# Two transformer blocks on one core: 258 columns, earlier splits, sums by fours and reordered steps

## Chip, core and metric

One core of one Trainium2 chip runs the kernel in a single launch. The metric is the device time of that launch in microseconds (us); lower is better. Three runs of the kernel before gave 1582.75, 1585.87 and 1586.20 us, so their median is 1585.87 us.

## What is computed

A sequence of 16 meta tokens and 256 input tokens of 1024 features passes through a first block of two layers. Then the 256 tokens pass through a second block of two more. All numbers are fp32. Cut to the shapes that matter:

```python
hs = concat([meta_tokens, x])                      # 272 tokens, first_block
for i in range(2):
    mix = gated_deltanet(...) if i == 0 else mlstm(...)
    hs = hs + rms_norm(mix, norm_w[i, 1])
    u = causal_depthwise_conv(rms_norm(hs, norm_w[i, 2]) @ w_up[i], conv_w[i]) + conv_b[i]   # 3 taps
    f = (silu(u[..., :2816]) * u[..., 2816:]) @ w_down[i]
    hs = hs + rms_norm(f, norm_w[i, 3])
x = hs[:, 16:]                                     # the meta tokens are dropped here
for layer in range(2):                             # second_block
    y = short_conv_mixer | swa_sink_attention  if layer == 0  else  gla_mixer | mla_mixer
    x = layer_norm(ALPHA * x + y @ w_out)
    x = layer_norm(ALPHA * x + (silu(x @ w_gate) * (x @ w_up)) @ w_down)
```

Nothing after the second layer's mixer mixes tokens except the convolution of three taps. For its 256 tokens the last projections of that layer need at most two tokens ahead of them.

## The kernel before

Activations lie with features on the partitions and tokens in the columns: 272 columns in the first block (`T1`), 256 in the second (`T2`), or 258 (`TB`) where two columns more carry a bias. All weights come as one stream of 412 blocks of 128 x 1024 fp32, loaded through SyncE's queue into a ring of four slots (`raw`). For each block ScalarE makes a rounded high part (`split_hi`, L375, `whi`) and VectorE the rest (`split_lo`, L380, `wlo`). TensorE then forms each fp32 product from three fp32r matmuls (`three`, L399 to L401): high by high, high by low, low by high. A block is 24 matmuls.

There are sixteen phases: an input projection (kind "tiles", one block gives one PSUM bank of 128 output features) and an output projection (kind "wide", each block adds to all eight banks) for each mixer and each feed-forward part. In order they are gdn_in, gdn_out, up0, down0, ml_in, ml_out, up1, down1, ev_in, ev_out, up2, down2, od_in, od_out, up3, down3. The names stand in the table `PHASES`.

The order on each engine is written out by hand, and semaphores join the engines. What the change touches:

- **The wave.** After a norm, `pe_tiles` starts the first three tiles of the next input projection while VectorE and ScalarE still produce its eight input chunks (`next_dve`, `next_act`, or `ln_dve`, `ln_act` in the second block). In the wave TensorE also sums squares over features with fp32 matmuls against ones (`sums_pe`, L565). VectorE first adds the squares in pairs (`pair_sum`, L621), so there are four such matmuls. `act_scale` (L505, L507) makes the scale from their sum.
- **The fourth and fifth tile.** The fourth tile's block is split inside the wave (`fourth`). The fifth's is split in `ffn_act`/`ffn_dve`, `ml_gates_act`/`ml_gates_dve` or `od_tile_act`/`od_tile_dve`, that is four tiles ahead (`TAIL = 4`).
- **The feed-forward pairs.** `ffn_act` and `ffn_dve` treat tiles two by two: scale, convolution taps (L690, L698) or bias, SiLU, product. GpSimd forms the gated product and its two parts (`ffn_pool`).
- **The mixers of the second block.** `even_pe`/`even_act`/`even_dve` lay tiles 6 to 17 of ev_in between the steps of the windowed attention. `odd_pe`/`odd_act`/`odd_dve`/`odd_pool` do so for od_in, the gated linear attention (gla) and the latent attention (mla).
- **The output rows.** `pe_wide` goes block by block. Each block passes all eight banks in order, and in the first block each bank is waited for (`bank_ready`), since the mixer's last steps still read some.

Of the kernel before, what the change touches and what calls it, by code (L numbers as in the profile page):

```python
# [42 lines left out]
OD_TILES = tuple(range(12, 17)) + (4, 5, 6, 7, 2, 3, 0, 1, 8, 9, 10, 11)  # L43
# [241 lines left out]
def build(nc, stream, params, consts, mla, hs_in, out, table):  # L285
# [98 lines left out]

    def split_all(engine, split, phase, lo=0, count=None):
# [17 lines left out]
    def pe_tiles(pe, phase, g0, name, count=None, meanwhile=lambda k: None):  # L403

        b0, n = FIRST_BLOCK[phase], count or COUNT[phase]
        T = width(phase)
        mm = nc.tensor.matmul

        for k in range(KC + 1):
            if k < KC:  # L410
                w = slice(k * P, (k + 1) * P)
                pe.wait_ge(*S("norm", "act").at(f"{name}_hi{k}"))
                for j in range(AHEAD):
                    o, s = rhs_out(g0 + j, phase), (b0 + j) % SLOTS
                    if k == 0:
                        pe.wait_ge(block_split, b0 + j + 1)
                        pe.wait_ge(bank_free, g0 + j + 1)
                    mm(o, whi[:, s, w], xs[:, k, 0:T], start=(k == 0), stop=False)  # L418
                    mm(o, wlo[:, s, w], xs[:, k, 0:T], start=False, stop=False)  # L419
            if k:  # L420
# [3 lines left out]
                for j in range(AHEAD):  # L424
                    last = mm(rhs_out(g0 + j, phase), whi[:, (b0 + j) % SLOTS, w], xs[:, KC + k - 1, 0:T], start=False, stop=(k == KC))  # L425
# [3 lines left out]
        def tile(j, i=0):  # L429
# [3 lines left out]
            for k in range(KC):  # L433
                last = three(rhs_out(g, phase), (b0 + j) % SLOTS, k, xs[:, k, 0:T], xs[:, KC + k, 0:T], k == 0, k == KC - 1)
# [27 lines left out]

    def pe_wide(pe, phase, g0, ready, bank_ready=lambda pe, b: None):

        b0, n = FIRST_BLOCK[phase], COUNT[phase]
        T = T1 if b0 < FIRST_BLOCK["ev_in"] else T2
        half = {"ml_out": range(ML_HALF, ML_HALF + 16), "od_out": OD_HALF}.get(phase, range(48))
        def rows(k, i=None):
# [4 lines left out]
            for m in range(8):  # L473
# [3 lines left out]
                last = three(rhs_out(g0 + m, phase), (b0 + k) % SLOTS, m, hf[:, half[at] if i is None else at, 0:T], hf[:, half[lo] if i is None else lo, 0:T], k == 0, k == n - 1)  # L477
                if i is None and k == n - 1 and m < 7:
                    last.then_inc(*S("wide", "pe").mark(f"{phase}_m{m}"))
            last.then_inc(block_used, 1)  # L480
# [8 lines left out]
        else:  # L489
            for k in range(n):  # L490
# [61 lines left out]
    def keep_clock(pe, g, n, lo=0):  # L552

        pe.wait_ge(bank_free, g + 1)
        for _ in range(n):
            nc.tensor.matmul(bank[g % 8][:, 0:T2], hf[:, lo, 0:P], hf[:, lo + 1, 0:T2], start=True, stop=True)

    def sums_pe(pe, name, src, g, parts, T):

        for m, first, last_one in parts:  # L560
# [4 lines left out]
            last = nc.tensor.matmul(bank[g % 8][:, 0:T], ones, ap, start=first, stop=last_one)  # L565
# [3 lines left out]
    def post_src(name):  # L569
        def src(m):  # L570
            return ("dve", f"{name}_sum{FIRST_SUM - 1}", sq[:, 0, :]) if m == 0 else ("act", f"{name}_{m}", sq[:, m, :])
        return src

    def post_pe(pe, name, g):
        sums_pe(pe, name, post_src(name), g, ((3, True, False), (4, False, False), (0, False, False), (5, False, False),
                                              (6, False, False), (7, False, True)), T1)
        keep_clock(pe, g + 1, 16, ML_HALF if name == "post2" else 0)

    def post_act(act, name, g, phase):
        for m in range(KC):  # L580
            wide_done(act, phase, m)
            nc.scalar.activation(sq[:, m, :], bank[(g - 8 + m) % 8][:, 0:T1], ACT.Square).then_inc(*S("norm", "act").mark(f"{name}_{m}"))  # L582
        split_hi(act, used_after(phase) + AHEAD - 1)
        act.wait_ge(*S("norm", "pe").at(name))
        nc.scalar.activation(rs[:, 1, :], bank[g % 8][:, 0:T1], ACT.Ln, bias=eps_1, scale=1.0 / D).then_inc(*S("norm", "act").mark(f"{name}_ln"))
        act.wait_ge(*S("norm", "act").at(f"{name}_ln"))
        nc.scalar.activation(rs[:, 1, :], rs[:, 1, :], ACT.Exp, scale=-0.5).then_inc(*S("norm", "act").mark(f"{name}_scale"))

    def post_dve(dve, name, g, row, split):
        v = S("norm", "dve")  # L590

        def scaled(m):
            dve.wait_ge(*S("norm", "act").at(f"{name}_{m}"))
            nc.vector.tensor_scalar(y[:, m, :], bank[(g - 8 + m) % 8][:, 0:T1], pv("norm_w", row * KC + m), None, ALU.mult).then_inc(bank_free, 1)
# [2578 lines left out]
```

## Time and profile before

| | |
|---|---|
| median of three runs | 1585.87 us |
| the profiled execution's own time | 1586.19 us |
| its span in the profile | 1584.4 us |
| TensorE busy | 1491.8 us, 94% |
| VectorE busy | 1045.4 us, 66% |
| ScalarE busy | 803.7 us, 51% |
| GpSimd busy | 253.7 us, 16% |
| read from HBM | 220.28 MB, 140 GB/s |

The busy time of TensorE counts matmuls that overlap in its pipeline, so a matmul's own duration says little: the spacing of their starts is what counts, and the windows show it. In rows of waits the engine at the left waited for the one at the right. L numbers are lines of the kernel before.

### The profile page before, as it was taken

The numbers are of one execution on the slowest core, as the hardware profiler recorded it, in microseconds if no ns is written. First come the engines' busy times: TensorE is split into PE (matmuls) and PEld (weight loads), VectorE is DVE, ScalarE is ACT, GpSimd is POOL, SyncE is SP. The second block draws the span as 40 slices with busy tenths as digits, with TensorE's granted clock in tenths as the row PEclk, the third lists the DMA queues.
The fourth block names the chain that finished last, engine by engine and source line by source line (L and its number), as shares of the span: only waits on it lengthen the run. The fifth ranks groups of instructions, "written<-read, shape, count | busy, mean of one in ns | idle before, by whom it ended". The sixth has DMA issues, their size and how long they took to land.

```text
span 1584.4 us, 32592 instructions
## 1 busy us (share of the span) xinstructions
PE 1491.8 (94%) x11761; PEld 1432.5 (90%) x11761; DVE 1045.4 (66%) x1743; ACT 803.7 (51%) x1392; POOL 253.7 (16%) x307
## 2 busy tenths in 40 slices
PE   6999969899999999999999998899999987999997
PEld 5997869698999998988999997899999976999996
DVE  4884874557888468557888466666664784676654
ACT  5555532446665356446655354454453664554443
POOL 0201200200555000000555000002210011022200
PEclk9998986999999999999999999999999998999999
DMA  5552220043555535333655533446555522365551
GB/s 200 179 178 80 94 80 2 1 147 99 194 176 182 173 120 164 104 117 105 190 179 174 179 121 132 130 137 197 181 168 197 174 84 81 107 195 180 184 184 54
DMA packets 61142, 222.56 MB, mean 140 GB/s; under 512 B 6784, under 2 KB 7808, under 8 KB 60672
## 3 DMA queue, kind: packets, MB, share of 16 engines
q1 hardware_dynamic: 60912, 220.17, 43.2%
q8 instruction: 61, 1.00, 0.3%
q10 hardware_dynamic: 144, 1.18, 0.2%
q14 instruction: 25, 0.20, 0.0%
HBM read 220.28 MB, written 1.05 MB: 140 GB/s over the span
## 4 chain that ended last, share of the span: by engine, by line
PE 81%; DVE 10%; ACT 5%; issue 2%; DMA 1%; ACTq 0%; DVEq 0%; SPq 0%
PE bank L399 22%; PE bank L400 21%; PE bank L401 21%; DVE wlo L380 2%; ACT whi L375 2%; PE bank L418 1%; PE bank L419 1%; PE bank L425 1%; PE bank L565 1%; PE bank L1879 1%; ACT sq L582 1%; PE bank L1220 1%; DMA par<-params 1%; PE bank L1200 1%; DVE y L2117 1%
## 5 line engine op out<-in xcount | busy, mean ns | idle before, releaser
L380 DVE TENSOR_TENSOR wlo<-raw,whi 128x1024 fp32r<-128x1024 f32 x412 | 516.7, 1255 | 309.4 <-ACT whi L375 308.2
L375 ACT ACTIVATE whi<-raw 128x1024 fp32r<-128x1024 f32 x412 | 434.4, 1056 | 376.7 <-PE bank L401 361.4
L399 PE MATMUL bank<-xs,whi 128*128 128x272 f32 (+2 forms) x2080 | 601.5, 289 | 13.7 <-DVE wlo L380 11.2
L400 PE MATMUL bank<-xs,whi 128*128 128x272 f32 (+2 forms) x2080 | 595.8, 286 | 0.0
L401 PE MATMUL bank<-xs,wlo 128*128 128x272 f32 (+2 forms) x2080 | 593.7, 285 | 0.0
L399 PEld LDWEIGHTS bank<-xs,whi 128*128 128x128 f32 x2080 | 394.4, 190 | 18.8 <-issue 14.7
L400 PEld LDWEIGHTS bank<-xs,whi 128*128 128x128 f32 x2080 | 394.7, 190 | 0.4 <-issue 0.2
L401 PEld LDWEIGHTS bank<-xs,wlo 128*128 128x128 f32 x2080 | 395.0, 190 | 0.0
L399 PE MATMUL bank<-hf,whi 128*128 (+2 forms) x1024 | 294.4, 287 | 7.3 <-DVE mix L2385 2.4
L400 PE MATMUL bank<-hf,whi 128*128 (+2 forms) x1024 | 293.0, 286 | 0.0
L401 PE MATMUL bank<-hf,wlo 128*128 (+2 forms) x1024 | 292.8, 286 | 0.0
L399 PEld LDWEIGHTS bank<-hf,whi 128*128 128x128 f32 x1024 | 194.4, 190 | 9.1 <-issue 5.9
L400 PEld LDWEIGHTS bank<-hf,whi 128*128 128x128 f32 x1024 | 194.5, 190 | 0.1
L401 PEld LDWEIGHTS bank<-hf,wlo 128*128 128x128 f32 x1024 | 194.4, 190 | 0.0
L698 DVE SCALAR_TENSOR_TENSOR cv<-bank,par,cv 128x271 f32<-128x271 f32 (+2 forms) x272 | 119.8, 491 | 31.9 <-ACT cv L690 31.9
L807 POOL CAST hf<-cv 128x272 f32 (+3 forms) x88 | 68.6, 780 | 442.3 <-DVE cv L786 435.1
L690 ACT ACTIVATE cv<-bank,par 128x272 f32<-128x272 f32 x120 | 64.8, 553 | 89.9 <-DVE bank L775 73.4
L775 DVE TENSOR_TENSOR bank<-bank,rs 128x272 f32<-128x272 f32 (+1 forms) x176 | 77.0, 437 | 40.0 <-PE bank L401 28.3
L803 POOL TENSOR_TENSOR cv<-cv 128x272 f32<-128x272 f32 x44 | 53.8, 1222 | 234.6 <-ACT cv L750 234.6
L809 POOL TENSOR_TENSOR hf<-cv,hf 128x272 f32 (+3 forms) x88 | 73.0, 830 | 16.4 <-POOL hf L807 15.5
L418 PE MATMUL bank<-xs,whi 128*128 128x272 f32 (+2 forms) x192 | 52.0, 300 | 4.0 <-ACT xs L656 3.0
L419 PE MATMUL bank<-xs,wlo 128*128 128x272 f32 (+2 forms) x192 | 49.4, 285 | 0.0
(462 smaller groups left out, 1470.1 us busy)
## 6 DMA issues: line engine op xcount, KB each, us to landing
raw<-stream SPq DMA_DIRECT2D x412, 512.0 KB, 3.6
con<-consts SPq DMA_DIRECT2D x1, 1284.5 KB, 7.7
big<-mla ACTq DMA_DIRECT2D x1, 1152.0 KB, 5.5
hs_sb<-hs SPq DMA_DIRECT2D x1, 1088.0 KB, 5.1
y_out<-hs_sb SPq DMA_DIRECT2D x8, 128.0 KB, 2.0
par<-params SPq DMA_DIRECT2D x1, 644.0 KB, 8.8
```

The source lines that it names most:

```text
L375: nc.scalar.activation(whi[:, s, :], raw[:, s, :], ACT.Copy).then_inc(hi_split, 1)
L380: nc.vector.tensor_tensor(wlo[:, s, :], raw[:, s, :], whi[:, s, :].bitcast(F32), ALU.subtract).then_inc(block_split, 1)
L399: nc.tensor.matmul(out_, whi[:, slot, w], hi, start=start, stop=False)
L400: nc.tensor.matmul(out_, whi[:, slot, w], lo, start=False, stop=False)
L401: return nc.tensor.matmul(out_, wlo[:, slot, w], hi, start=False, stop=stop)
L418: mm(o, whi[:, s, w], xs[:, k, 0:T], start=(k == 0), stop=False)
L419: mm(o, wlo[:, s, w], xs[:, k, 0:T], start=False, stop=False)
L690: nc.scalar.activation(cv[:, slot, :], bk[:, 0:T1], ACT.Identity, **args).then_inc(*steps_.mark(f"{tag}{a}"))
L698: ins = nc.vector.scalar_tensor_tensor(o[:, tap:T1], bk[:, 0:T1 - tap], w[:, taps - 1 - tap:taps - tap], o[:, tap:T1], ALU.mult, ALU.add)
L775: nc.vector.tensor_tensor(u, u, rs[:, 0, 0:T], ALU.mult).then_inc(*st.mark(f"u{f}_{base}_{j}{a}"))
L807: nc.gpsimd.tensor_copy(hi, h).then_inc(*st.mark(f"hi{f}_{base}_{j}"))
L809: nc.gpsimd.tensor_tensor(lo, h, hi.bitcast(F32), ALU.subtract).then_inc(conv_taken, 2)
```

## The change

1. **258 columns.** From ml_out on, the output side of layer two is done for the last 258 or 256 tokens only: ml_out, its norm and up1 for columns 14 to 271, down1 and its norm for columns 16 to 271.
2. **The fifth tile.** It is split inside `act_scale`, between the logarithm and the exponential, and at the end of `next_dve` and `ln_dve`. The feed-forward pairs work five tiles ahead (`FFN_TAIL = 5`), and do both splits after their own products. `ml_gates_*` and `od_tile_*` are shifted to match.
3. **Sums by fours.** VectorE adds two pairs into one, so the wave has two matmuls against ones and not four. The last layer norm of all takes the eight squares directly.
4. **Steps reordered** in the even and the odd layer. od_in's tiles come in another order.
5. **Output rows joined.** In ml_out, ev_out and od_out the first two or three blocks are done together, bank group by bank group.

```diff
+    CONV_HALO = 2
+    FIRST_TOKEN = {"ml_out": N_META - CONV_HALO, "up1": N_META - CONV_HALO, "down1": N_META}
+    def cols(phase):
+        return slice(FIRST_TOKEN.get(phase, 0), width(phase))
...
-                    mm(o, whi[:, s, w], xs[:, k, 0:T], start=(k == 0), stop=False)
+                    mm(o, whi[:, s, w], xs[:, k, T], start=(k == 0), stop=False)
...
+    FIRST_ROWS = {"ml_out": (2, (range(5), range(5, 8))), "ev_out": (2, (range(2, 8), range(2))), "od_out": (3, (range(4, 6), range(4), range(6, 8)))}
...
-            for k in range(n):
+            together, groups = FIRST_ROWS.get(phase, (0, ()))
+            for ms in groups:
+                for k in range(together):
+                    rows(k, None, ms, ms is groups[-1])
+            for k in range(together, n):
                 rows(k)
...
         nc.scalar.activation(dst, bank[g % 8][:, lo:T], ACT.Ln, bias=eps, scale=1.0 / count).then_inc(bank_free, 1)
+        meanwhile()
         act.wait_ge(bank_free, 8 + g + 1)
...
         nc.vector.tensor_tensor(sq[:, m, lo:T], sq[:, m - 1, lo:T], sq[:, m, lo:T], ALU.add).then_inc(*v.mark(f"{name}_pair{m}"))
+        if m % 4 == 3:
+            dve.wait_ge(*v.at(f"{name}_pair{m}"))
+            nc.vector.tensor_tensor(sq[:, m, lo:T], sq[:, m - 2, lo:T], sq[:, m, lo:T], ALU.add).then_inc(*v.mark(f"{name}_four{m}"))
...
             scaled(0)
-            split_lo(dve, b0 + t + TAIL, ii)
             scaled(1)
...
+            split_lo(dve, b0 + t + FFN_TAIL, ii)
+            split_lo(dve, b0 + t + 1 + FFN_TAIL, ii)
...
         nc.scalar.preload_act_table_set(SIGMOID)
+        split(1)
         act.wait_ge(block_used, FIRST_BLOCK["ml_in"] + 1)
...
         if j < EV_FIRST + 2:
-            pe.wait_ge(bank_free, 8 + G["ev_out"])
+            pe.wait_ge(bank_free, 8 + G["ev_in"])
...
-        tile(10)
+        od_product(dve, 10)
         mla_weights(dve, 0)
-        keys(2, 3)
-        tile(11)
         mla_weights(dve, 1)
+        od_product(dve, 11)
+        od_low(dve, 10)
+        od_low(dve, 11)
...
-        for k in range(KC):
-            ln_wave(3)(k)
+        last_square = lambda m: ("act", f"ln3v_{m}", sqt(m))
+        sums_pe(pe, "ln3v", last_square, G["lv3"], [(m, m == 0, m == KC - 1) for m in range(KC)], T2)
```

**How the order moves.** The first place is ScalarE between the wave of up0 and its first pairs. L505 and L507 are the logarithm and the exponential of the scale (L526 and L529 after), L375 a split (L376 after), L690 the first tap (L720 after). Before:

```order
L505 ACTIVATE rs<-bank,con_eps 128x272
L507 ACTIVATE rs<-rs 128x272
L3028 ACT_TABLE_LOAD
...
L375 ACTIVATE whi<-raw 128x1024
...
L690 ACTIVATE cv<-bank,par 128x272
```

After:

```order
L526 ACTIVATE rs<-bank,con_eps 128x272
L376 ACTIVATE whi<-raw 128x1024
L529 ACTIVATE rs<-rs 128x272
L3073 ACT_TABLE_LOAD
...
L720 ACTIVATE cv<-bank,par 128x272
```

The fifth tile's split has moved ahead of the exponential and of the table load.

The second place is VectorE in the odd layer, after the maxima of the latent attention. L2965 to L2969 divide the weights by their sum (L3010 to L3014 after), L2532 and L2535 make the keys of the linear attention (L2573 and L2576 after; GpSimd multiplies them further in L2820), L2211 scales a tile (L2243 after). Before:

```order
L2211 TENSOR_TENSOR bank<-bank,rs 128x256
L380 TENSOR_TENSOR wlo<-raw,whi 128x1024
L2965 TENSOR_REDUCE work<-work 128x4
L2967 RECIPROCAL work<-work 128x4
L2969 TENSOR_TENSOR work<-work 128x512
L2532 TENSOR_TENSOR y<-big 128x2x256
L2535 TENSOR_SCALAR y<-y 128x2x256
...
L380 TENSOR_TENSOR wlo<-raw,whi 128x1024
L2965 TENSOR_REDUCE work<-work 128x4
L2967 RECIPROCAL work<-work 128x4
L2969 TENSOR_TENSOR work<-work 128x1024
```

After:

```order
L2243 TENSOR_TENSOR bank<-bank,rs 128x256
L3010 TENSOR_REDUCE work<-work 128x4
L3012 RECIPROCAL work<-work 128x4
L3014 TENSOR_TENSOR work<-work 128x512
L3010 TENSOR_REDUCE work<-work 128x4
L3012 RECIPROCAL work<-work 128x4
L3014 TENSOR_TENSOR work<-work 128x1024
L2243 TENSOR_TENSOR bank<-bank,rs 128x256
L381 TENSOR_TENSOR wlo<-raw,whi 128x1024 x2
```

The keys and the splits no longer stand between the two normalisations: the keys have moved ahead, the splits behind.

The third place is ScalarE at the end of the odd layer. L2714 and L2718 load tables (L2753 and L2765 after), L2717 is the SiLU of the gate, L2721 squares the outputs (L2764 after). Before:

```order
L2714 ACT_TABLE_LOAD
L2717 ACTIVATE big<-big 128x4x256
L2718 ACT_TABLE_LOAD
L2721 ACTIVATE sq<-bank 128x256 x4
```

After:

```order
L2753 ACT_TABLE_LOAD
L376 ACTIVATE whi<-raw 128x1024
...
L2758 ACTIVATE big<-big 128x3x256
...
L2761 ACTIVATE big<-big 128x256
L2764 ACTIVATE sq<-bank 128x256 x4
L2765 ACT_TABLE_LOAD
```

One load now stands before tile 15, the other behind the squares.

## Rows read from the trace of the kernel before

**Rows 1.** The page: busy time of each engine.

```profile
PE 1491.8 (94%) x11761; PEld 1432.5 (90%) x11761; DVE 1045.4 (66%) x1743; ACT 803.7 (51%) x1392; POOL 253.7 (16%) x307
```

**Rows 2.** Windows of up1, down1, up2, down2: us, PE busy, clock, DMA share, GB/s.

```profile
739.71:865.41 125.70, 123.78 (x987) 1.00 0.57 178
865.41:932.35 66.94, 66.70 (x531) 1.00 0.55 177
1056.09:1175.45 119.36, 117.81 (x987) 1.00 0.58 188
1175.45:1239.07 63.62, 62.88 (x531) 1.00 0.56 182
```

**Rows 3.** Waits of TensorE: us in total, times, longest us.

```profile
PE bank L399 <- DVE wlo L380: 11.2, 9, 2.0
...
PE bank L2891 <- DVE work L2969: 7.0, 2, 5.7
PE bank L2590 <- ACT sq L2721: 5.7, 1, 5.7
PE bank L2250 <- DVE work L2428: 5.4, 2, 3.9
...
PE bank L399 <- DVE mix L2385: 2.4, 1, 2.4
PE bank L399 <- ACT big L2176: 2.3, 1, 2.3
...
PE bank L399 <- DVE mix L2020: 1.6, 1, 1.6
...
PE bank L399 <- DVE cv L786: 1.5, 2, 0.7
PE bank L399 <- DVE sq L2800: 1.4, 1, 1.4
```

**Rows 4.** Windows in the even and odd layers where the clock was halved, columns as in rows 2.

```profile
974.50:977.90 3.40, 2.82 (x13) 0.50 0.22 60
1018.90:1022.30 3.40, 3.40 (x19) 0.50 0.38 149
1309.00:1315.90 6.90, 5.78 (x27) 0.51 0.23 72
1339.80:1346.60 6.80, 4.41 (x12) 0.50 0.20 73
```

**Rows 5.** Timeline of ScalarE at the start of up0: start, us, engine, line, operation.

```profile
385.65 0.49 ACT L505 ACTIVATE rs<-bank,con_eps 128x272 f32<-128x272 f32 x1 [2.09 <-PE bank L565]
```

**Rows 6.** Timeline of VectorE and of TensorE there.

```profile
384.04 1.22 DVE L380 TENSOR_TENSOR wlo<-raw,whi 128x1024 fp32r<-128x1024 f32 x1
...
384.15 0.62 PE L565 MATMUL bank<-sq,con 128*128 128x272 f32 x2
...
384.99 0.62 PE L565 MATMUL bank<-sq,con 128*128 128x272 f32 x2
```

**Rows 7.** Timeline of ScalarE in the gates of ml_in.

```profile
600.44 0.51 ACT L1730 ACTIVATE work<-work,par 4x272 f32<-4x272 f32 x1
...
604.58 1.99 ACT L375 ACTIVATE whi<-raw 128x1024 fp32r<-128x1024 f32 x2
```

**Rows 8.** Timeline of GpSimd and VectorE between the normalisations of the odd layer.

```profile
1298.58 3.37 POOL L2820 TENSOR_TENSOR y<-y,big 128x512 f32<-128x512 f32 x2 [58.81 <-ACT big L2202]
...
1300.73 1.77 DVE L2532 TENSOR_TENSOR y<-big 128x512 f32<-128x512 f32 x1
...
1302.87 0.68 DVE L2532 TENSOR_TENSOR y<-big 128x512 f32<-128x512 f32 x1
...
1307.38 1.21 DVE L2965 TENSOR_REDUCE work<-work 128x4 f32<-128x1024 f32 x1
```

**Rows 9.** Timeline of ScalarE in the last norm.

```profile
1570.82 1.08 ACT L2103 ACTIVATE sq<-y 128x256 f32<-128x256 f32 x3 [11.99 <-DVE y L2140]
...
1576.60 0.47 ACT L505 ACTIVATE rs<-bank,con_eps 128x256 f32<-128x256 f32 x1 [1.31 <-PE bank L565]
```

More of the change, by code:

```diff
@@ L383, in fourth, with fifth @@
         return FIRST_BLOCK[phase] + AHEAD
+    def fifth(phase):
+        return FIRST_BLOCK[phase] + AHEAD + 1
     def split_all(engine, split, phase, lo=0, count=None):
@@ L433, in tile @@
             for k in range(KC):
-                last = three(rhs_out(g, phase), (b0 + j) % SLOTS, k, xs[:, k, 0:T], xs[:, KC + k, 0:T], k == 0, k == KC - 1)
+                last = three(rhs_out(g, phase), (b0 + j) % SLOTS, k, xs[:, k, T], xs[:, KC + k, T], k == 0, k == KC - 1)
             last.then_inc(block_used, 1)
@@ L448, in width @@
         return TB if phase in ("up2", "od_in", "up3") else T2
+    CONV_HALO = 2
+    FIRST_TOKEN = {"ml_out": N_META - CONV_HALO, "up1": N_META - CONV_HALO, "down1": N_META}
+    POST_FIRST = {"post0": 0, "post1": 0, "post2": FIRST_TOKEN["ml_out"], "post3": FIRST_TOKEN["down1"]}
+    PRE_FIRST = {"pre1": 0, "pre2": 0, "pre3": FIRST_TOKEN["up1"]}
+    FFN_FIRST = (0, FIRST_TOKEN["up1"], 0, 0)
+    FFN_OUT = (0, FIRST_TOKEN["down1"], 0, 0)
+    def cols(phase):
+        return slice(FIRST_TOKEN.get(phase, 0), width(phase))
     def rhs_out(g, phase):
-        return bank[g % 8][:, 0:width(phase)]
+        return bank[g % 8][:, cols(phase)]
     def wide_done(engine, phase, m):
@@ L472, in rows @@
             ready(pe, k, i)
-            for m in range(8):
+            for m in ms:
                 if k == 0 and i is None:
@@ L476, in rows @@
                     bank_ready(pe, (g0 + m) % 8)
-                last = three(rhs_out(g0 + m, phase), (b0 + k) % SLOTS, m, hf[:, half[at] if i is None else at, 0:T], hf[:, half[lo] if i is None else lo, 0:T], k == 0, k == n - 1)
+                last = three(rhs_out(g0 + m, phase), (b0 + k) % SLOTS, m, hf[:, half[at] if i is None else at, T], hf[:, half[lo] if i is None else lo, T], k == 0, k == n - 1)
                 if i is None and k == n - 1 and m < 7:
                     last.then_inc(*S("wide", "pe").mark(f"{phase}_m{m}"))
-            last.then_inc(block_used, 1)
+            if done:
+                last.then_inc(block_used, 1)
         if n == 22:
@@ L564, in sums_pe @@
             pe.wait_ge(*S("norm", who).at(mark))
-            last = nc.tensor.matmul(bank[g % 8][:, 0:T], ones, ap, start=first, stop=last_one)
+            last = nc.tensor.matmul(bank[g % 8][:, lo:T], ones, ap, start=first, stop=last_one)
         if last_one:
@@ L2106, in ln_act @@
         act.wait_ge(bank_free, 8 + g + 1)
-        act_scale(act, name + "v", g + 1, rs[:, 0, 0:T2], T2, D, eps_ln)
+        act_scale(act, name + "v", g + 1, rs[:, 0, 0:T2], T2, D, eps_ln, meanwhile=lambda: split_hi(act, fifth(phase)) if phase else None)
     def ln_dve(dve, n, which, layer, phase, wide, split):
@@ L2145, in ln_dve @@
                 lo(m - 1)
-            if m % 2 == 0 and m:
+            if phase and m % 2 == 0 and m:
                 pair_sum(dve, name + "v", m - 1, T2)
```

234 lines of the change are left out of this document (125 added, 109 removed).

## The prediction

> **What bounds the kernel now.** I read the page first. TensorE is busy for 94% of the span and VectorE, the next, for 66% [rows 1], so TensorE's matmuls and the gaps between them are the time. Second come the windows by phase. up1 takes 125.70 us with TensorE busy for 123.78, and up2, with the same number of matmuls on 256 or 258 columns, 119.36 with 117.81; down1 and down2 differ in the same way [rows 2]. Columns thus cost time almost in full. Third are TensorE's waits: the reader should see that none is for a DMA of weights, and that most end with a split, a normalisation or squares on VectorE or ScalarE [rows 3]. Fourth are stretches of the two mixers in which the granted clock is 0.50 or 0.51, the lower of the two levels (1.2 GHz) [rows 4]. TensorE had waited in or just ahead of each. Its busy time there is twice what full clock needs, so half of 2.82, 3.40, 5.78 and 4.41 us could be saved. Last are timelines, for what stands in a row where a part changes.
>
> The sum is made against the profiled execution's own 1586.19 us, 0.32 above the median of the runs. A measurement of this kernel tells 0.2% (3.2 us) from no change.
>
> **Columns.** up1's busy time should become up2's: 123.78 - 117.81 = 6.0. down1 follows down2: 66.70 - 62.88 = 3.8 [rows 2]. ml_out has 8 blocks, 192 matmuls of the same shape as up1's 987, and 192 x 6.0 / 987 = 1.2. The norms between lose some columns too, 0.5 by my estimate. Together **-11.5**. If VectorE could not follow, up1 would keep its 125.70; that is a rival.
>
> **Rows joined in ml_out.** The wait for L2020, 1.6, is for the sixth bank of the first block. With five banks times two blocks ahead of it, it is ready. **-1.6** [rows 3].
>
> **Starts of up0 and up1.** Of TensorE's 11.2 us of waits for L380 [rows 3], all but 1.8 lie at the fourth to sixth tile behind a wave: 1.9 in up0, 1.6 in up1, 2.0 in ml_in, 1.6 each in up2 and up3, 0.8 in od_in. In up0, a sum and three fp32r matmuls follow one another at 0.84 (384.15 to 384.99), so the wave leads into the fourth tile at 385.83, and the logarithm stands at 385.65 [rows 5, 6]. Now ScalarE splits the fifth tile right behind that, and VectorE does its part at once, so its stall falls to about 0.1. VectorE pays two adds more, which delay the fourth tile's low part (384.04, 1.22 long [rows 6]) beyond the third tile: +0.4. Net -1.4 for up0, and -1.1 for up1, where the pairs' taps leave a stall of about 0.4: **-2.5**. Its bounds are 0 (the splits queue elsewhere) and -3.5.
>
> **ml_in.** Its 2.0 goes, but the split now stands ahead of the row copies and of the low gate rows. The chain of the gates (600.44 to the splits at 604.58, 4.1 us [rows 7]) starts 1.4 later by one split of 1.0 and a part of the other, and two tiles and the first step of the mixer sit behind its end. I take 3.4 lost for 2.0 won: **+1.4**, between -2 and +3.5.
>
> **up2, up3.** Here the wave is paced by TensorE, so each fp32 sum that goes gives back its price. That is 0.84 less three matmuls of 0.127, or 0.46 (rather 0.41 for 256 columns) [rows 6]: 0.8 for two. The stall falls from 1.6 to about 0.4. Twice 2.0 is **-4.0**. down2 and down3 start without the 1.5 for L786 [rows 3], as the product now stands ahead of the splits: **-1.5**.
>
> **The last norm.** The first square starts at 1570.82 and is done 0.4 later; the logarithm starts at 1576.60 [rows 9]. Between them VectorE alternates adds of pairs with its own chunks. Without them eight sums of 0.41 to 0.46 follow the first square at 1571.24, ending at 1574.9: **-1.6**.
>
> **Even layer.** The wait for L2176 (2.3) goes: tile 6 no longer stands behind a bank. Of 3.9, the longer for L2428, a split of 1.0 and one of 1.2 leave the chain and 1.7 stays; of the other 1.5, 0.5. The 2.4 for L2385 falls to the joined rows of ev_out [rows 3]. That makes 2.3 + 2.2 + 1.0 + 2.4 = 7.9. The halved stretches give back (2.82 + 3.40) / 2 = 3.1 [rows 4]. From 11.0 I keep **-10**, since a reordered chain leaves a new small wait somewhere.
>
> **Odd layer.** VectorE's work between the two normalisations, from 1300.73 to 1307.38 [rows 8], has moved away. So the longer wait for L2969, 5.7, goes; of the other, 1.3, a part of 0.8. Of the 5.7 for L2721 I leave 2.3: one table load and the four last logarithms' worth still stand ahead, where two loads and a SiLU stood. The wait for L2800, 1.4, goes, as od_out starts with the banks that are free [rows 3]. The two stretches give (5.78 + 4.41) / 2 = 5.1 [rows 4], and the start of od_in gives 0.8 for two sums and 0.5 of its stall. Sum: 5.7 + 0.8 + 3.4 + 1.4 + 5.1 + 1.3 = 17.7.
>
> Against it stands what the keys meet in their new place. One at 1300.73 took 1.77 beside GpSimd's multiplies, which ran from 1298.58 to 1301.95; one of the same shape at 1302.87, with GpSimd idle, took 0.68 [rows 8]. VectorE's operation ended 0.55 after GpSimd's did, so it seems to have been held whole. All four keys and multiplies are now in the stretch before the maxima. By these rows one meeting costs 1.1, and in the worst case a GpSimd multiply's 1.7 each, 6.8 for four. I take two meetings, +2, and **-15.7**. The Trainium skill, "SBUF — State Buffer", section "SBUF: two separate sides", calls the port pair that VectorE and GpSimd share an exclusive lock, under which whichever starts second is blocked for the whole instruction, if VectorE's reads two inputs in SBUF; by that rule it is the four times 1.7, and the sum would end 4.8 higher. The row above agrees with the rule for one meeting.
>
> **Sum.** -11.5 - 1.6 - 2.5 + 1.4 - 4.0 - 1.5 - 1.6 - 10 - 15.7 = -47.0, so 1586.2 - 47.0 = **1539.2**. A quarter of it is columns, more than a half is the two mixers and rests on nothing else being late there.
>
> **Rivals.**
> *The mixers find a new wait.* On the odd layer's new order, VectorE makes all keys beside GpSimd's multiplies ahead of the maxima. If the normalisation comes 4 to 7 us late again and the clock drops again (2.9 from the first stretch [rows 4]), it gives 1539 + 7 to 1539 + 10: 1546 to 1549. For it: 1.77 against 0.68 [rows 8]. Against: TensorE has tiles between to cover some of it. Chance 0.2.
> *VectorE becomes the bound in up1.* Its columns then bring nothing, and the pairs' splits queue: 1539 + 6 = 1545. Against: up2 does the same work in 119.36, with 1.55 of idle TensorE [rows 2]. Chance 0.1.
> *Slower: the offset of the columns.* The matmuls of ml_out and up1 now read 258 columns from column 14, 56 bytes into a row; none in the trace does so. If such a read were fed at the fp32 pace, 0.46 / 2 = 0.23 a matmul in place of 0.12 [rows 6], the 192 + 987 matmuls would take 0.11 x 1179 = 130 us more: 1669. It decides above 47 / 1179 = 0.04 per matmul. Against: the columns still follow one another in each row, and only the start moves; no row speaks on it. Chance 0.04.
> *The change does not do what it says* (joined rows and reordered steps wait for the same banks, and the half clock stays): only columns and starts remain, 1586 - 20 = 1566. Chance 0.04; no change at all, 0.02.
>
> **How the numbers follow.** My forecast, 1539.2, has 0.6; its own range is 1531 to 1548 by the bounds above (the even layer 7 to 12, the odd 11 to 19, the starts -2 to +3). The rivals have 0.2, 0.1, 0.04, 0.04 and 0.02. The range from 1530 to 1552 takes in the first two rivals and their own spread and leaves out about a tenth at either end. Faster by over 0.2% are all cases but the slower one, no change, and a sliver for an unnamed mishap: 0.93. The same: 0.02. Slower: 0.05.
>
> **What would show it.** In the windows up1 should read about 119.5 to 120 and down1 63.6. TensorE's waits for L380 should sum to 3 to 4 in place of 11.2. The waits after both normalisations (L3014 now) should be under 1 each, the one for the squares (L2764) near 2.3, and those at L2385's and L2800's places gone. The clock should stay at 1.00 in the even and the odd layer. In ml_in a wait behind the gates' chain should have grown by 3.4. The forecast is wrong if a stretch at 0.50 still stands in the odd layer, if the keys take 1.8 each, or if up1 has gaps for VectorE.

## The result and the profile after

The change brought the median from 1584.31 us (four runs) to **1550.2 us** (four runs, 1548.2 to 1551.5). The ratio on record is 0.977, with a 95% interval from 0.9752 to 0.9787 (the quotient of these two medians alone is 0.9785). The forecast was 1539.2 with a range from 1530 to 1552: the time lies inside it, near its upper end, and 34 to 36 us were won where 47 were forecast. The profiled execution took 1549.72 us, with a span of 1547.9, so 36.5 us of span went. One execution of one kernel below (the one without joined rows) ran at a clock of 0.65 throughout, took 2042 us, and is left out everywhere.

The page of the changed kernel: span and busy time. L numbers are from here on lines of the kernel that a row comes from.

```profile
span 1547.9 us, 32593 instructions
...
PE 1475.3 (95%) x11745; PEld 1417.8 (92%) x11745; DVE 1048.4 (68%) x1751; ACT 795.9 (51%) x1393; POOL 280.5 (18%) x307
```

TensorE's waits after, to be read against [rows 3]: what waited, for what, us in total, times, longest.

```profile
...
PE bank L403 <- DVE cv L728: 9.0, 2, 4.9
PE bank L403 <- DVE wlo L381: 5.8, 6, 3.0
PE bank L422 <- ACT xs L686: 5.0, 9, 0.8
...
PE bank L2289 <- DVE work L2469: 2.5, 2, 1.6
...
PE bank L403 <- ACT sq L2768: 1.8, 1, 1.8
PE bank L2936 <- DVE work L3014: 1.8, 1, 1.8
...
PE bank L1879 <- DVE work L2067: 0.3, 1, 0.3
PE bank L2631 <- ACT sq L2764: 0.3, 1, 0.3
```

Most of [rows 3] has shrunk: 11.2 for splits became 5.8, 7.0 for the normalisations 1.8, 5.7 for the squares 0.3, and 2.4, 2.3 and 1.6 are gone. The 1.4 at the start of od_out did not go. It became 1.8 and waits for the squares' logarithms on ScalarE (L2768). And there is a row of 9.0 that nobody forecast. TensorE waits twice, 4.1 and 4.9 us, for L728, the convolution's taps. Before there were two such waits of 0.2.

The most useful view is a ledger by stretch. A stretch runs from the first matmul of a wave to that of the next; its times come from the timelines of TensorE in the two profiled executions.

| stretch (from the start of its wave) | before | after | moved | forecast |
|---|---|---|---|---|
| to up0, the first mixer | 373.96 | 371.63 | -2.3 | 0 |
| up0, down0 | 209.93 | 215.21 | **+5.3** | -1.4 |
| ml_in, ml_out | 143.94 | 142.67 | -1.3 | -1.4 |
| up1, down1 | 209.85 | 208.46 | **-1.4** | -11.4 |
| ev_in, ev_out | 107.95 | 96.01 | -11.9 | -10 |
| up2, down2 | 197.09 | 193.84 | -3.2 | -2.8 |
| od_in, od_out | 131.56 | 114.68 | -16.9 | -15.7 |
| up3, down3, last norm | 210.12 | 205.42 | -4.7 | -4.3 |

Six stretches came out as forecast or a little better, together 6 us better than the plan. The two first feed-forward parts fell 16.7 us short of it. Windows of the changed kernel show where: the tiles of up0, down0, the tiles of up1, down1, and the first 5.3 us of each output projection after its wait (columns: stretch and its us, busy time of PE, PEld, DVE, ACT and POOL, then clock, DMA share, GB/s).

```profile
384.02:508.11 124.09, 123.69 (x985) 123.45 (x985) 103.34 (x166) 71.88 (x107) 63.51 (x60) 1.00 0.56 174
508.11:586.84 78.73, 73.80 (x558) 72.91 (x556) 38.33 (x47) 32.17 (x41) 5.66 (x6) 0.96 0.53 165
741.51:862.35 120.84, 120.31 (x985) 118.80 (x986) 100.41 (x164) 70.33 (x106) 61.88 (x60) 1.00 0.58 178
862.35:937.97 75.62, 69.99 (x558) 69.18 (x557) 38.49 (x49) 32.42 (x41) 5.51 (x6) 0.95 0.55 173
514.70:520.00 5.30, 5.30 (x23) 5.30 (x24) 2.30 (x2) 1.43 (x2) 2.40 (x3) 0.50 0.40 143
869.70:875.00 5.30, 5.30 (x25) 5.30 (x26) 2.29 (x2) 1.42 (x2) 2.33 (x3) 0.50 0.42 128
```

up0's tiles did get faster: the same stretch was 125.72 before. What they won, and more, went in down0: a wait of 4.1 and then 5.3 us at half clock, which cost another 2.65. In down1 it is 4.9 and 2.65.

The timeline of VectorE at the end of up0 in the changed kernel shows who is late.

```profile
507.14 1.78 DVE L728 SCALAR_TENSOR_TENSOR cv<-bank,par,cv 128x271 f32<-128x271 f32 x4 [0.36 <-ACT cv L720]
508.84 1.22 DVE L381 TENSOR_TENSOR wlo<-raw,whi 128x1024 fp32r<-128x1024 f32 x1
510.37 1.40 DVE L381 TENSOR_TENSOR wlo<-raw,whi 128x1024 fp32r<-128x1024 f32 x1 [0.32 <-ACT whi L376]
511.69 0.78 DVE L806 TENSOR_TENSOR bank<-bank,rs 128x272 f32<-128x272 f32 x2
512.83 1.78 DVE L728 SCALAR_TENSOR_TENSOR cv<-bank,par,cv 128x271 f32<-128x271 f32 x4 [0.36 <-ACT cv L720]
```

TensorE ended up0's last tile at 508.1, and VectorE came to scale it only at 512.0. It was not waiting for TensorE at any point in these rows: its gaps are for ScalarE's tap and split. From one set of taps to the next (507.14 to 512.83) this last pair takes it 5.7 us, and nearly all pairs before it took 5.98. TensorE takes 2 x 124.09 / 41 = 6.05 for two tiles of 272 columns.

That gave the theory for the experiments, **deferred debt**: in up0 and up1 the chain of VectorE and ScalarE needs about as long for a pair as TensorE does; it starts late, since the wave keeps it busy; a stall taken from the start of the phase is only owed until its end, where TensorE waits once for all of it, with the clock's fall on top. The rivals were that VectorE's work alone sets the phase's length, and that only the order of the last splits is to blame.

Part of this theory holds, and the timelines of VectorE tell which. Behind the stalls, when TensorE ends up0's sixth tile (397.2 before, 393.7 after), VectorE comes to scale it 4.0 us later before the change and 5.0 after (401.20, 398.65). So the removed stall adds only 1 us to the lateness. The other 4 us were there before, and were worked off within the phase. What differs is the time of a pair. The taps of two pairs in a row in up0, before and after:

```profile
413.67 1.31 DVE L698 SCALAR_TENSOR_TENSOR cv<-bank,par,cv 128x271 f32<-128x271 f32 x3 [0.60 <-ACT cv L690]
...
419.20 1.31 DVE L698 SCALAR_TENSOR_TENSOR cv<-bank,par,cv 128x271 f32<-128x271 f32 x3 [0.60 <-ACT cv L690]
```

```profile
429.62 1.78 DVE L728 SCALAR_TENSOR_TENSOR cv<-bank,par,cv 128x271 f32<-128x271 f32 x4 [0.65 <-ACT cv L720]
...
435.60 1.79 DVE L728 SCALAR_TENSOR_TENSOR cv<-bank,par,cv 128x271 f32<-128x271 f32 x4 [0.65 <-ACT cv L720]
```

Before, a pair took VectorE 5.52 us while it was behind. It gained 0.5 on TensorE's 6.0 with each, was level after some ten pairs, and then took TensorE's 6.01 and waited for it. After, a pair takes 5.98 in up0, so hardly anything is gained in 22 pairs. In up1 it takes 5.87, and TensorE could do a pair of 258 columns in 5.73 (its pace with four tiles ahead, below), so there VectorE sets the pace. VectorE's waits in up0's tiles, before (386 to 511) and after (384 to 508):

```profile
DVE cv L698 <- ACT cv L690: 12.3, 21, 0.6
DVE bank L775 <- PE bank L401: 4.2, 11, 0.4
DVE wlo L380 <- ACT whi L375: 2.0, 2, 1.7
```

```profile
DVE cv L728 <- ACT cv L720: 13.3, 21, 0.7
DVE wlo L381 <- ACT whi L376: 7.5, 21, 1.1
```

Before, a split stood between the two scalings of a pair and another behind the taps. Now both stand behind the taps, and VectorE waits in every pair for ScalarE's part of the second. So by these rows it is the place of the splits inside the pair that takes VectorE's slack away, while most of its lateness stems from ahead of the phase. No run changes that place alone and keeps five tiles ahead.

### The profile page after: what moved, and what is told of

Same layout as the page of the kernel before. It is cut to its first block, busy times and chain, and to the rows that moved or that the text cites. A ratio compares the mean times of both kernels' runs of the same rounds, so it can differ in the third digit from the quotient of the medians.

```text
span 1547.9 us, 32593 instructions
## 1 busy us (share of the span) xinstructions
PE 1475.3 (95%) x11745; PEld 1417.8 (92%) x11745; DVE 1048.4 (68%) x1751; ACT 795.9 (51%) x1393; POOL 280.5 (18%) x307
## 4 chain that ended last, share of the span: by engine, by line
PE 66%; DVE 15%; ACT 9%; issue 7%; DMA 1%; DVEq 1%; ACTq 1%; SPq 0%
PE bank L403 17%; PE bank L404 17%; PE bank L405 17%; ACT whi L376 4%; DVE wlo L381 3%; DVE cv L728 2%; DVE bank L806 2%; ACT cv L720 2%; PE bank L422 1%; PE bank L429 1%; PE bank L423 1%; PE bank L1908 1%; PE bank L587 1%; ACT sq L607 1%; PE bank L1250 1%
## 5 line engine op out<-in xcount | busy, mean ns | idle before, releaser
L403 PE MATMUL bank<-xs,whi 128*128 128x258 f32 (+2 forms) x2080 | 601.0, 289 | 6.1 <-DVE wlo L381 5.8
L404 PE MATMUL bank<-xs,whi 128*128 128x258 f32 (+2 forms) x2080 | 593.6, 285 | 0.0
L405 PE MATMUL bank<-xs,wlo 128*128 128x258 f32 (+2 forms) x2080 | 591.2, 284 | 0.0
L376 ACT ACTIVATE whi<-raw 128x1024 fp32r<-128x1024 f32 x412 | 432.7, 1056 | 291.0 <-PE bank L405 282.8
L403 PE MATMUL bank<-hf,whi 128*128 (+3 forms) x1024 | 294.0, 287 | 10.8 <-DVE cv L728 9.0
L404 PE MATMUL bank<-hf,whi 128*128 (+3 forms) x1024 | 292.6, 286 | 0.0
L405 PE MATMUL bank<-hf,wlo 128*128 (+3 forms) x1024 | 292.5, 286 | 0.0
L403 PEld LDWEIGHTS bank<-hf,whi 128*128 128x128 f32 x1024 | 195.6, 191 | 11.9 <-DVE cv L728 9.4
L728 DVE SCALAR_TENSOR_TENSOR cv<-bank,par,cv 128x271 f32<-128x271 f32 (+4 forms) x272 | 117.7, 488 | 34.8 <-ACT cv L720 34.7
L837 POOL CAST hf<-cv 128x256 f32 (+3 forms) x88 | 67.6, 768 | 383.8 <-DVE cv L814 376.4
L720 ACT ACTIVATE cv<-bank,par 128x272 f32<-128x272 f32 (+1 forms) x120 | 59.6, 546 | 100.8 <-DVE bank L806 84.8
L839 POOL TENSOR_TENSOR hf<-cv,hf 128x256 f32 (+3 forms) x88 | 99.9, 1136 | 16.6 <-POOL hf L837 15.6
L833 POOL TENSOR_TENSOR cv<-cv 128x272 f32<-128x272 f32 (+1 forms) x44 | 53.2, 1209 | 234.8 <-ACT cv L779 234.8
L806 DVE TENSOR_TENSOR bank<-bank,rs 128x256 f32<-128x256 f32 (+2 forms) x176 | 69.8, 426 | 5.6 <-PE bank L405 5.3
L422 PE MATMUL bank<-xs,whi 128*128 128x258 f32 (+2 forms) x192 | 52.1, 300 | 6.1 <-ACT xs L686 5.0
## 6 DMA issues: line engine op xcount, KB each, us to landing
raw<-stream SPq DMA_DIRECT2D x412, 512.0 KB, 3.7
```

The lines of the kernel that those rows point to most:

```text
L376: nc.scalar.activation(whi[:, s, :], raw[:, s, :], ACT.Copy).then_inc(hi_split, 1)
L403: nc.tensor.matmul(out_, whi[:, slot, w], hi, start=start, stop=False)
L404: nc.tensor.matmul(out_, whi[:, slot, w], lo, start=False, stop=False)
L405: return nc.tensor.matmul(out_, wlo[:, slot, w], hi, start=False, stop=stop)
L422: mm(o, whi[:, s, w], xs[:, k, T], start=(k == 0), stop=False)
L720: nc.scalar.activation(cv[:, slot, lo:T1], bk[:, lo:T1], ACT.Identity, **args).then_inc(*steps_.mark(f"{tag}{a}"))
```

## The experiments

All are edits of the changed kernel, which is at 1550.2 (span 1547.9). Ratios are to the kernel before; those medians were 1586.6, 1586.55 and 1586.16 in the three batches.

### Four tiles ahead again in up0 and up1

```diff
             scaled(0)
+            if f < 2:
+                split_lo(dve, b0 + t + TAIL, ii)
             scaled(1)
             if f < 2:
                 conv_rest(...)
+                split_lo(dve, b0 + t + 1 + TAIL, ii)
+                return
```

The same on ScalarE, and the fifth tile of up0 and up1 isn't split early. So the splits also go back to their old places inside the pair. up2 and up3 stay five ahead.

> Theory (deferred debt): in up0 and up1 VectorE needs as long for a pair as TensorE does, so the stall taken from the start of the phase is only owed until its end, where down0 and down1 wait 4.1 and 4.9 us for the last taps and the clock drops. With the pairs of up0 and up1 at four tiles ahead again, the waits of 4.1 and 4.9 fall under 0.6 each and the halved clock behind them (about 2.6 us each) goes, while about 1.9 us of stalls return at each start: 8 to 10 us less than the changed kernel's 1550, so 1540 to 1542. Rival (VectorE's work alone sets the length of up0 and up1, wherever the splits stand): the waits move to the start and nothing is gained, 1549 to 1551.

Measured: **1537.2 us** (1535.8 to 1539.8), ratio 0.9688 [0.9666, 0.9711], 13 us less than the changed kernel and more than expected. Windows of the same four parts:

```profile
385.14:510.59 125.45, 123.87 (x985) 123.45 (x985) 105.32 (x170) 76.98 (x110) 66.47 (x62) 1.00 0.54 178
510.59:582.94 72.35, 71.33 (x558) 70.43 (x556) 34.64 (x42) 29.91 (x37) 4.08 (x4) 1.00 0.51 170
737.58:857.44 119.86, 118.17 (x984) 117.76 (x985) 102.75 (x170) 76.20 (x109) 64.56 (x62) 1.00 0.57 186
857.44:925.88 68.44, 67.38 (x558) 66.67 (x556) 34.26 (x42) 29.56 (x36) 3.98 (x4) 1.00 0.54 180
```

down0 is 6.4 us shorter and down1 7.2, at full clock, for 1.4 us in up0's tiles. up1's tiles got 1.0 shorter although their start stalls again. VectorE at the end of up0 now waits for TensorE (0.60) before it scales the last tile:

```profile
508.96 1.23 DVE L381 TENSOR_TENSOR wlo<-raw,whi 128x1024 fp32r<-128x1024 f32 x1 [0.28 <-ACT whi L376]
510.79 0.45 DVE L807 TENSOR_TENSOR bank<-bank,rs 128x272 f32<-128x272 f32 x1 [0.60 <-PE bank L405]
```

A pair takes VectorE 5.52 us in up0 and 5.41 in up1 while it is behind, and TensorE's 6.01 and 5.73 once it is level. The rival that VectorE's work alone decides falls, since that work is the same. The 1.9 us of stalls came back only in part, 1.6 and 1.7.

### One tap left out, five tiles ahead kept

```diff
-                conv_rest(..., tiles, i, 3, FFN_FIRST[f])
+                conv_rest(..., tiles, i, 2, FFN_FIRST[f])
```

> The changed kernel with five tiles ahead, but the convolution's third tap is left out in up0 and up1 (output changed on purpose of the test: two operations of 0.4 us fewer per pair on VectorE). Theory (deferred debt): VectorE now has 0.8 us of slack in each of 22 pairs, catches up long before the end, and the waits of 4.1 and 4.9 at the start of down0 and down1 fall under 0.6 with no halved clock behind them, though the splits stand exactly where they stood: 1535 to 1538. Rival (it is the order at the end alone, the two splits queued ahead of the last pair's taps): waits of 2.5 and more stay, 1543 to 1547.

The third tap of the convolution is missing in up0 and up1, so this kernel doesn't compute the block.

Measured: 1532.8 us (1530.0 to 1535.7), ratio 0.9658 [0.9633, 0.9682]; the wait for L728 is gone. The windows of up0's tiles, down0, up1's tiles, down1:

```profile
385.04:508.63 123.59, 123.59 (x984) 123.40 (x985) 94.70 (x128) 73.27 (x109) 73.21 (x63) 1.00 0.57 182
508.63:580.48 71.85, 71.06 (x558) 70.38 (x556) 34.08 (x41) 30.36 (x38) 3.75 (x4) 1.00 0.54 170
735.10:853.17 118.07, 117.91 (x985) 117.71 (x986) 95.46 (x128) 70.55 (x109) 70.35 (x62) 1.00 0.61 189
853.17:921.13 67.96, 67.21 (x558) 66.66 (x556) 33.72 (x41) 29.90 (x37) 4.38 (x4) 1.00 0.57 181
```

This is the run that decides between the theory and the order of the last splits. The splits stand exactly where the change put them, and with 0.8 us less of VectorE's work per pair (a pair takes it 5.57 us in up0 and 5.50 in up1) the two waits and the half clock vanish. So five tiles ahead is not wrong as such: it pays where VectorE has slack in each pair to catch up in. up2 and up3, which have no taps, show the same in the changed kernel, where their tiles went from 119.35 to 117.97.

### The end of the phase: joined rows, and the last pair first

The first edit joins the first two blocks of down0 and down1 over six banks before the two last; the second puts the last pair's taps ahead of two splits and adds pair sums (below) and the joined rows.

```diff
+            two = int(phase in ("down0", "down1"))
+            for ms in (range(6), range(6, 8)) if two else (range(8),):
+                for k in range(1 + two):
+                    rows(k, None, ms, ms[-1] == 7)
```

> The first two blocks of down0 and of down1 are done together over six banks before the two last ones. Theory (deferred debt): TensorE gets 18 more matmuls, 2.3 us, ahead of each wait for the last taps, and VectorE ends at the same moment, so the waits fall from 4.1 and 4.9 to about 1.9 and 2.7: 4.4 us less, and up to 5 more if the clock no longer halves, so 1541 to 1546. Rival (TensorE's second block itself comes late, since its split is queued behind): the wait becomes one for a split, and no more than 1 us is gained, 1549.

Measured: 1542.75 us, ratio 0.9725 [0.9702, 0.9749]. The waits for the taps fell from 9.0 to 4.3:

```profile
PE bank L403 <- DVE cv L731: 4.3, 2, 2.4
```

Some half clock stayed behind each (0.60 over the first 3.1 us in down0, 0.50 over the first 3.0 in down1), so each of the two stretches got 3.2 us shorter, 6.4 together.

> Five tiles ahead, but the last pair's taps stand before two of the last splits, the first two blocks of down0 and down1 are joined, and waves behind rms norms sum by pairs. Theory (the debt can be hidden by other work of TensorE at the end): the taps end 1.2 to 1.6 earlier and 2.3 us more matmuls cover them, so the waits of 4.1 and 4.9 fall under 1, no clock is lost, and the early start is kept: 1534 to 1537, at least as fast as four tiles ahead. Rival (whatever is taken out of the end appears as a wait for a split of the second or third block): 1540 to 1544.

Measured: 1536.94 us (1535.1 to 1538.8), ratio 0.969 [0.967, 0.971]. One wait for the taps is left, at down1, of 0.5, and the clock is 1.00 in both places; the starts of up0 and up1 stall for 0.8 and 1.0. The up0 and down0 stretch is the shortest of all with the full computation, 208.5 (210.2 with four ahead, 209.9 with four ahead and pair sums), but up1 and down1 take 201.6 against 200.0. So VectorE's lateness can be hidden under other work at the end too. In up1, where its pair still takes 5.86 against TensorE's 5.73, not being late is better.

### Sums by pairs behind the rms norms

```diff
-        if m % 4 == 3:
+        if m % 4 == 3 and name[:3] != "pre":
...
-        in_wave = lambda name: fours_in_wave(...)
+        in_wave = lambda name: pairs_in_wave(...)
```

> The three waves behind rms norms sum by pairs again (four matmuls against ones, two adds fewer on VectorE each); the layer norms keep fours. Theory: VectorE paces these waves, so up0's, ml_in's and up1's get 0.4 to 0.5 us shorter, and the waits at the start of down0 and down1 fall by about the two adds, 0.9 each: 1.5 to 3.3 less, 1547 to 1549. Rival (TensorE's sums are the price): the waves get 0.5 to 0.9 longer each, 1552.

Measured: 1548.23 us, ratio 0.9751 [0.973, 0.9772]. The waves got shorter by what was expected: 12.39 to 11.87 in up0, 12.30 to 11.87 in ml_in, 12.00 to 11.40 in up1. The second half of the expectation failed: the waits for the taps stayed at 9.0. The sign of the fours thus depends on who paces the wave. VectorE paces these; TensorE paces the layer norms' waves, which went from 10.46 to 9.60 by the fours.

> Pairs of up0 and up1 at four tiles ahead, and sums by pairs in the waves behind rms norms, the two together. Theory: the parts add, 1537.2 less 0.5 in each of the waves of up0, ml_in and up1: 1535.6. Rival (with four ahead the earlier end of the wave only meets a longer stall for the split): 1537.2 as without pairs.

Measured: 1535.53 us (1534.4 to 1536.8), ratio 0.968 [0.9657, 0.9703]. The two parts add within what these runs tell; a difference of 1.7 from 1537.2 is near the spread of the medians. Each wave shows its 0.5, and ml_in's tiles took 103.3 in this profile, with a wait of 1.5 at the mixer's start and a stretch at a clock of 0.89 behind it, which may be chance.

### All 272 columns, with five and with four tiles ahead

```diff
-    FIRST_TOKEN = {"ml_out": N_META - CONV_HALO, "up1": N_META - CONV_HALO, "down1": N_META}
+    FIRST_TOKEN = {"ml_out": 0, "up1": 0, "down1": 0}
```

> All 272 columns in ml_out, up1 and down1, the rest as changed. Theory (VectorE paces up1, so its columns bring little there): ml_out +1.2, down1 +3.8, norms +0.5, up1 only 2 to 3, that is +8, 1558. Rival (columns are worth their full busy time, as predicted): +11.5, 1561.7.

Measured with five ahead: 1556.33 us, ratio 0.9805 [0.9784, 0.9825].

> Four tiles ahead in up0 and up1, and all 272 columns in ml_out, up1 and down1. Theory (with VectorE no longer in debt the columns are worth what their busy time says): 1537.2 + 6 (up1) + 3.8 (down1) + 1.2 (ml_out) + 0.5 = 1548.7; with five ahead the same columns brought 6 (1556.3 against 1550.2). Rival (VectorE paces up1 at four ahead too): up1's tiles give 2 to 3, 1545.

Measured with four ahead: 1546.98 us, ratio 0.9754 [0.9736, 0.9772]. up1's tiles with 272 columns, five and four ahead:

```profile
742.22:866.23 124.01, 123.64 (x985) 123.42 (x986) 103.35 (x166) 71.80 (x107) 63.48 (x60) 1.00 0.54 175
738.25:863.68 125.43, 123.88 (x985) 123.46 (x985) 105.37 (x170) 76.96 (x110) 66.18 (x62) 1.00 0.57 178
```

The fewer columns save 1556.3 - 1550.2 = 6.1 with five ahead and 1547.0 - 1537.2 = 9.8 with four. In spans it is 6.6 and 10.3. In up1's tiles alone it is 124.01 - 120.84 = 3.2 and 125.43 - 119.86 = 5.6. The change's own second part thus took over a third of what its first part brought.

### The old order in the even and in the odd layer

Each run puts the even or the odd layer's steps (and od_in's tiles) back as they stood, and keeps the joined rows and the sums.

```diff
-            pe.wait_ge(bank_free, 8 + G["ev_in"])
+            pe.wait_ge(bank_free, 8 + G["ev_out"])
...
-            if j < 14:
-                split_lo(dve, b0 + j + TAIL)
+            split_lo(dve, b0 + j + TAIL)
...
         weights(1)
-        masked(2)
         taps(0)
         tile(10)
+        masked(2)
```

> The changed kernel with the even layer's steps in the old order (output rows still joined). Theory (the reordering and the clock account for the gain of that layer): its stretch gets 8 to 10 of its 11.9 us back, the waits for L2469 grow to 3.9 and 1.5 and that behind tile 6 to 2.3, with the halved clock behind: 1558 to 1560. Rival (the gain came from the wave and the joined rows): at most 4 back, 1554.

Measured: 1558.44 us, ratio 0.9827 [0.9804, 0.985]. The tiles of ev_in take 69.0 and not 60.3 (67.8 before), and the waits are back:

```profile
PE bank L2289 <- DVE work L2467: 5.4, 2, 3.9
...
PE bank L403 <- ACT big L2207: 2.5, 1, 2.5
```

So 8.7 of the layer's 11.9 come back with the old order. Some 1.2 of them are clock that the kernel before did not lose: over 965 to 985 it is 0.83 here and was 0.91 there. The output projection keeps all it had won, 26.5 against 30.8 before, although the steps are old. Joined rows alone are thus enough to take away the wait of 2.4 at its start.

```diff
-        od_product(dve, 10)
+        tile(10)
         mla_weights(dve, 0)
+        keys(2, 3)
+        tile(11)
         mla_weights(dve, 1)
-        od_product(dve, 11)
-        od_low(dve, 10)
-        od_low(dve, 11)
```

> The changed kernel with the odd layer's steps and tiles in the old order (output rows still joined, sums by fours). Theory (the reordering and the clock account for it): 12 to 15 of 16.9 us come back, with a wait of 5 to 6 for the second normalisation, one of 4 to 6 for the squares and two stretches at half clock: 1562 to 1565. Rival (the joined rows and the sums carry it): at most 8 back, 1558.

Measured: 1563.78 us, ratio 0.9857 [0.9833, 0.9882], that is 13.6 more. od_in's tiles take 92.1 and not 76.9. Both waits are back at their old size:

```profile
PE bank L2931 <- DVE work L3009: 7.3, 2, 5.7
...
PE bank L2630 <- ACT sq L2761: 5.7, 1, 5.7
```

od_out takes 26.6 here with its rows joined, and took 28.9 before.

### The early split in ml_in taken back

Four ahead and pair sums, and the fifth tile of ml_in with its gates in the old order:

```diff
         nc.scalar.preload_act_table_set(SIGMOID)
-        split(1)
...
+        split(0)
+        split(1)
```

> Four ahead and pairs as in the run before, and the fifth tile of ml_in and its gates in the old order too. Theory (in ml_in the early split delays the chain of the gates by more than it saves, as predicted): the stretch of ml_in's tiles goes from 101.6 back to 100.4, 1534 to 1534.5. Rival (it makes no difference there): 1535.5.

Measured: 1535.99 us (1532.9 to 1537.7), ratio 0.9676 [0.9655, 0.9697]. In total this can't be told from the 1535.53 with the early split. In the trace the tiles of ml_in take 100.42, as before the change (100.42), against 101.56 in the changed kernel and in six of the other runs. The wait for the fifth tile's split, 2.0, stands there again in place of the later one of 3.0 (in the changed kernel at 608.12 to 611.45), and a wait of 1.5 stands at the mixer's start, as before the change and as in the run with the early split (0.3 in the changed kernel).

### No rows joined

```diff
-    FIRST_ROWS = {"ml_out": ..., "ev_out": ..., "od_out": ...}
+    FIRST_ROWS = {}
```

> The changed kernel with no output rows joined. Theory (joined rows take the place of the waits at the start of ml_out, ev_out and od_out, each with its own price): ml_out +1.6, ev_out +2.4 to 5 (a wait and its clock), od_out +1.4 to 4: 1555 to 1560. Rival (the reordered steps have already freed the banks): under 1.5 in all, 1551.

Measured: 1551.52 us, ratio 0.9778 [0.9761, 0.9796], which can't be told from 0.977. It has no profile to read. The expectation of 1555 to 1560 failed. Joining the rows brings about 1.3 us in the changed kernel, within what these runs tell from nothing. In the even layer either edit takes the wait away by itself: joined rows do so with the old steps (above), and by the total here the new steps do too, since 1.3 us leaves no room for the 4 us that the wait and its clock cost in ev_out before. In ml_out other runs show the gain: with its rows joined and all 272 columns it takes 29.8, and took 31.7 before.

### The fastest kernel

Of those that compute everything, the kernels at 1535.5 and 1536.0 us are the fastest and beat both kernels of the case. They keep the change but for four tiles ahead in up0 and up1 and pairs in the waves behind rms norms. By the stretches, five ahead with the reordered end in up0 alone would give about 1.4 us more; that wasn't tried.

## Why the prediction was right, and where it was wrong

**Columns, -11.5.** The matmuls did become faster as forecast: down1 runs at down2's pace, and no price of the offset of 56 bytes is to be seen, so that rival is out. With four tiles ahead up1's matmuls start 0.1194 us apart in the timeline, and up2's, which begin at column 0, 0.1195. But the term held only where VectorE kept up. Four ahead it measures 9.8 to 10.3, five ahead 6.1 to 6.6. The failed step is "if VectorE could not follow", which was given 0.1. The reason against it was up2's small idle time, and up2 has no taps: the row that was chosen didn't have the work in question. In this the named rival, that VectorE becomes the bound in up1, came true in part: its pair takes 5.87 us against TensorE's 5.73. [Rows 1] gave VectorE 66%, and it was busy for 105 of 126 us in up0. A busy share doesn't show how much slack a pair has, since VectorE and ScalarE wait for each other inside it: VectorE's busy time in up0 fell from 105 to 103 us, and its pair grew from 5.52 to 5.98. The pair's period is what must be laid beside TensorE's.

**Starts of up0 and up1, -2.5.** Mechanism right, bounds wrong. The stalls at the start went from 1.9 in each to 0.4 and 0.5 (the prediction read 1.6 for up1 and 1.8 for the first mixer, where the trace has 1.9 and 1.5), and up0's tiles won 1.6 us. The step that failed is "Its bounds are 0 and -3.5". It asked what is late at the start, and not what the splits' new place does to each of the 22 pairs and so to the end. The measured price of the edit in these two phases is 13 us (1550.2 against 1537.2), 5.3 of it clock and some 4 of it columns. The prediction had priced the split's place for its neighbours only.

**up2, up3, down2, down3, the last norm: -7.1.** Measured -3.2 and -4.7, or 7.9. Two sums fewer gave 0.86 in each wave against 0.8 (10.46 to 9.60), and the tiles 1.4 against 1.2.

**The wave's fours behind rms norms, +0.4 each.** Measured +0.5 in up0 and +0.4 in ml_in; in up1, with fewer columns, +0.6 by the run with pair sums.

**Rows joined in ml_out, -1.6, and its columns, -1.2.** ml_out went from 31.7 to 28.8; with all 272 columns and joined rows it took 29.8, so 1.9 is the rows and 1.0 the columns.

**ml_in, +1.4.** Measured +1.1 in its tiles (100.42 to 101.56). The wait moved from the fifth tile (2.0) to the sixth (3.0), for a forecast of 3.4.

**Even layer, -10.** Measured -11.9. The waits for L2428 were forecast at 1.7 and 0.5 and are 1.6 and 0.8; those for L2176 and L2385 are gone. The term kept 1 us for a new wait that did not come. The 2.4 had been put down to the joined rows; the joined rows alone do take it away, and by the total of the run without them the reordered steps do too.

**Odd layer, -15.7.** Measured -16.9. Of the two normalisations the wait for the second is gone and that for the first, 1.3 before, is 1.8 (forecast 0.5). Of the squares 0.3 is left (forecast 2.3), but od_out starts with the wait of 1.8 for their logarithms, for which the forecast had nothing; together that is 2.1 against 2.3. Against the forecast the clock did not stay at 1.00: it is 0.65 over 3.6 us behind that wait (the row is shown in the last section), and 0.52 from 1316.5 to 1319.0. A stretch at 0.50 in the odd layer had been named as a sign that the forecast is wrong. The two GpSimd meetings, +2, were right in size and wrong in what they held:

```profile
1271.10 1.64 DVE L381 TENSOR_TENSOR wlo<-raw,whi 128x1024 fp32r<-128x1024 f32 x1 [0.24 <-ACT whi L376]
1272.66 0.68 DVE L2573 TENSOR_TENSOR y<-big 128x512 f32<-128x512 f32 x1
1273.37 1.39 DVE L2576 TENSOR_SCALAR y<-y 128x512 f32<-128x512 f32 x1
1274.68 0.68 DVE L2573 TENSOR_TENSOR y<-big 128x512 f32<-128x512 f32 x1
```

```profile
1270.25 1.41 POOL L2865 TENSOR_TENSOR y<-y,big 128x512 f32<-128x512 f32 x1 [45.38 <-ACT y L2559]
1273.20 1.28 POOL L2865 TENSOR_TENSOR y<-y,big 128x512 f32<-128x512 f32 x1 [1.54 <-ACT y L2559]
1275.50 1.47 POOL L2865 TENSOR_TENSOR y<-y,big 128x512 f32<-128x512 f32 x1 [1.02 <-ACT y L2559]
```

All four keys took 0.68. Three of them met no multiply, and the one at 1272.66 had begun before one. The L2576 that began at 1273.37 behind a multiply (1273.20) took 1.39 and not 0.43, and ended 0.28 after it. Two splits that began behind other multiplies (1271.10 and 1276.40) took 1.64 and 1.65 and not the 1.21 of one with GpSimd idle. That is 1.8 in all. The rule of the Trainium skill ("SBUF — State Buffer", section "SBUF: two separate sides"), that whoever starts first keeps the shared port pair, agrees with who was held. It names VectorE's instructions with two inputs in SBUF, as the splits have, and those in a 2-port mode; L2576 reads one tensor, and no row shows its mode. The prediction had charged the keys, by counting overlaps and not who starts first. The rival that the mixers find a new wait of 4 to 7 us did not come.

**The sum.** Outside up0 to down1, the terms were -34.2 and the trace gives -40.4, of which 2.3 lie ahead of up0, where the change does next to nothing: the first mixer's stretch took 351.7 before, 349.6 after, and 350.3 to 352.1 in the runs of the other kernels with the same code, so this is a difference between executions. In up0, down0, up1 and down1, -12.8 was forecast and +3.9 measured. The time lies inside the range, whose upper end is 13 us above the middle, and that is luck in part: this end had been drawn for the mixers and for up1's columns alone, and 6 us won elsewhere beyond the plan made up for part of the 16.7 that were missing.

## What to carry to other kernels

An engine that follows the leader through a long phase, and starts it late, gets level only if it has slack in each period. An edit that moves its work inside the period can take that slack away without adding any work; then the lateness stays to the phase's end, where it comes in one piece and takes the clock with it. So before pricing such an edit, lay the follower's period per unit (from one group of its instructions to the same group one unit on, its waits for third engines included) beside the leader's, and look at what the last unit must finish before the next phase can start. A row from a similar phase serves only if it has the same work in it.

## What was not expected of the hardware

After the 4.1 us wait TensorE ran at half clock for about 5.3 us. In three other runs with the same wait and the same code behind it (all columns, old even layer, old odd layer) the clock over those 5.3 us was 0.68 or 0.69, and down0 took 77.8 and not 78.7, so 1 us of the +5.3 in the ledger is a difference between executions. After waits of 1.9 and 2.4 in the run with joined rows some of it stayed, and after one of 0.5 none. In the changed kernel's od_out a wait of 1.8 was followed by a stretch at 0.65, and so in two other runs; in eight runs the same wait, with the same code behind it, was followed by none, which makes 1.5 us of difference between executions:

```profile
1314.40:1318.00 3.60, 3.60 (x21) 3.60 (x22) 3.45 (x10) 2.64 (x8) 0.00 (x0) 0.65 0.02 5
```

The wait that is left for the first normalisation varied too, from 1.4 to 3.1 us over runs in which the odd layer's code was the same. What it hangs on wasn't found.
